# Selected values travel with the NSA pages, four MoBA columns among the pairs, transposes parted

## What is computed

```python
z = x @ w_in                       # one projection, split among four head groups
# A  conformer convolution (256 channels)
# B  native sparse attention, 4 heads, one K/V head per branch:
kc, vc = nsa_compress(rows[:, :, 0]), nsa_compress(rows[:, :, 1])   # compressed branch
# selected branch: blocks of 64 rows of rows[:, :, 2:] (sel_k, sel_v), top 16 by importance
# window branch: the last 512 rows and the row itself
# C  MoBA, 4 heads, blocks of 256 keys, top 3 and the own block
# D  multi-scale causal pooling
x = LN(ALPHA * x + concat(A, B, C, D) @ w_out)
x = LN(ALPHA * x + relu(x @ w_up)**2 @ w_down)
```

## Time and profile before

| | us |
|---|---|
| median of 3 runs | 766.06 (770.39, 765.99, 766.06) |
| profiled execution, device time | 770.32 |
| its span in the profile | 768.6 |
| PE busy | 737.8 |
| DVE busy | 429.2 |
| ACT busy | 285.5 |
| POOL busy | 210.4 |

### The profile page before, as it was taken

One profiled execution on the slowest core, in us unless ns is written; L12 is line 12 of the kernel. 1 busy time (PEld: TensorE's weight loads), 2 busy tenths in 40 slices (PEclk: granted clock), 3 DMA queues, 4 the chain that ended last, 5 costly groups with the idle time before them and its releaser, 6 DMA issues.

```text
span 768.6 us, 17343 instructions
## 1 busy us (share of the span) xinstructions
PE 737.8 (96%) x6904; PEld 659.2 (86%) x6904; DVE 429.2 (56%) x740; ACT 285.5 (37%) x561; POOL 210.4 (27%) x284
## 2 busy tenths in 40 slices
PE   8999999998987899999999999999999999999997
PEld 7999989875563545589999999999999999999996
DVE  4878994665643532556866556433563355536355
ACT  5222334465553222533434454212341124324115
POOL 0000527024226772004747721001110012100433
PEclk9999999999999899999999999999999999999999
DMA  9656773378779996321332333322233323325002
GB/s 332 188 151 182 213 200 97 133 286 315 280 252 309 261 280 208 117 83 56 130 144 84 89 104 104 117 83 84 83 104 93 106 71 95 107 87 165 2 15 99
DMA packets 63980, 113.49 MB, mean 148 GB/s; under 512 B 17017, under 2 KB 36218, under 8 KB 63226
## 3 DMA queue, kind: packets, MB, share of 16 engines
q1 hardware_dynamic: 57370, 95.58, 39.9%
q0 software_dynamic: 6528, 16.78, 6.7%
HBM read 107.90 MB, written 6.52 MB: 149 GB/s over the span
## 4 chain that ended last, share of the span: by engine, by line
PE 76%; DVE 8%; DMA 5%; issue 5%; SPq 4%; ACT 3%; POOL 0%; ACTq 0%; DVEq 0%; POOLq 0%
PE psum L793 55%; DMA moba_hi<-in_moba_pages 4%; PE psum L812 4%; PE psum L820 3%; PE psum L899 2%; PE psum L933 2%; SPq L707 1%; PE psum L1085 1%; SPq L629 1%; PE psum L868 1%; PE psum L1097 1%; DVE yc L1700 1%; DVE wL L1630 1%; PE psum L1133 1%; DMA wgate<-in_w_gate 1%
## 5 line engine op out<-in xcount | busy, mean ns | idle before, releaser
L1630 DVE TENSOR_TENSOR wL<-raw,wH 128x1024 fp32r<-128x1024 f32 (+1 forms) x85 | 107.1, 1261 | 84.2 <-ACT wH L1258 84.2
L1258 ACT ACTIVATE wH<-raw 128x1024 fp32r<-128x1024 f32 (+1 forms) x87 | 88.8, 1021 | 103.1 <-PE psum L793 101.1
L793 PE MATMUL psum<-oxH,wH 128*128 128x260 f32 (+1 forms) x512 | 105.0, 286 | 0.7 <-DVE oxL L2054 0.5
L793 PE MATMUL psum<-oxH,wL 128*128 128x260 f32 (+1 forms) x512 | 103.9, 284 | 0.0
L793 PE MATMUL psum<-oxL,wH 128*128 128x260 f32 (+1 forms) x512 | 103.4, 283 | 0.0
L1592 POOL TENSOR_TENSOR hsq<-relu 128x520 f32<-128x520 f32 x32 | 33.8, 1055 | 217.9 <-ACT relu L1437 217.9
L793 PE MATMUL psum<-opH,wH 128*128 128x260 f32 x400 | 85.5, 295 | 5.2 <-DVE wL L1630 1.4
L793 PEld LDWEIGHTS psum<-oxH,wH 128*128 128x128 f32 x512 | 79.5, 189 | 2.5 <-issue 1.7
L793 PE MATMUL psum<-opL,wH 128*128 128x260 f32 x400 | 80.5, 283 | 0.0
L793 PE MATMUL psum<-opH,wL 128*128 128x260 f32 x400 | 80.5, 283 | 0.0
L793 PEld LDWEIGHTS psum<-oxL,wH 128*128 128x128 f32 x512 | 79.9, 190 | 0.0
(11 more groups left out here) (395 smaller groups left out, 1313.1 us busy)
## 6 DMA issues: line engine op xcount, KB each, us to landing
raw<-in_panels SPq DMA_DIRECT2D x88, 512.0 KB, 3.6
nsa_ring<-in_nsa_pages SPq DMA_DIRECT2D x128, 96.0 KB, 2.2
moba_hi<-in_moba_pages SPq DMA_DIRECT2D x36, 256.0 KB, 5.2
moba_lo<-in_moba_pages SPq DMA_DIRECT2D x36, 256.0 KB, 5.3
moba_hi<-in_moba_pages POOLq DMA_DIRECT2D x28, 256.0 KB, 5.1
moba_lo<-in_moba_pages POOLq DMA_DIRECT2D x28, 256.0 KB, 5.5
xres<-in_xT SPq DMA_DIRECT2D x8, 260.0 KB, 5.2
xres<-in_xT SPq DMA_DIRECT2D x1, 2080.0 KB, 8.6
```

The source lines that it names most:

```text
L793: last = mm(out[:, hf, 0:cols], w, x[:, k, hf * HALF:hf * HALF + cols], start=(t == 0 and j == 0), stop=(t == KT - 1 and j == 2))
L1258: fn(wtiles(0, n).rearrange("p a b -> p (a b)")[:, cols], raw[:, n % NRAW, cols], ACT.Copy).then_inc(h_done, 1)
L1630: tt(wtiles(1, n).rearrange("p a b -> p (a b)")[:, cols], raw[:, n % NRAW, cols], wtiles(0, n).rearrange("p a b -> p (a b)")[:, cols].bitc ...
```

## The change

- `nsa_pages` grows to 256 columns: the selected values ride with the pages. w1's reserve shrinks from 16384 to 8192 bytes a partition, so the larger ring ends where it ended.
- In step `("nsa", b)` ACT first waits for the pages and copies their last 64 columns into `stage` (two buffers over `Vn` and `zs`); POOL writes `stage` (512 KB) to an internal DRAM tensor, `selv_rows[b]`. The next load into the ring waits for the copy too.
- `("selv", b)` is one load of 512 KB by SP, one for each sample, 5 units of time apart; POOL loads none.
- `zcols`, which fills `Vn`, waits for all write-backs; the convolution's temporary moves to `taps_tmp`.
- `NAHEAD` = 22: columns 18 to 21 (MoBA, first pair of heads) move among the pairs. They use banks 4 and 5 alone; from column 22 on odd columns use banks 0 and 3.
- `("st", b, 1)` is due 1.6 units after `("st", b, 0)`, not 2.5, and `("spv", b)` at 5.9, not 6.5. With the denser columns the merged order has other steps between the transposes.
- `comb_sub` and `comb_exp` become one semaphore.

```diff
+NAHEAD = sum(c[0] != "moba" for c in COLS) + 4
 def col_banks(n):
-    return (0, 3) if COLS[n][0] == "moba" and n % 2 else (4, 5)
+    return (0, 3) if n >= NAHEAD and n % 2 else (4, 5)
...
-MB1, PAIR_T, SELV_T = 9, 9.1, 6
-SELV_POOL = (1, 3, 5, 7)
-SELV_AT = [8 * (_m // 8) + (_m % 8) // 2 + 4 * (_m % 2) for _m in range(4 * B)]
-NCN = sum(c[0] != "moba" for c in COLS)
+MB1, PAIR_T, SELV_T = 9, 9.1, 5
...
         units += [(at_, ("mu", g)), (at_ + 2.5, ("mt", g)), (at_ + 4.7, ("mp", g))]
-        units += [(at_ + 4.6 * (m >= 4), ("selv", k)) for m, k in enumerate(SELV_AT[SELV_T * (g - MB1):SELV_T * (g - MB1 + 1)])]
     end = 1 + PAIR_T * (MB - MB1)
+    units += [(1 + SELV_T * b, ("selv", b)) for b in range(B)]
...
-        join += [(at_ - 3, ("psc", b))] + [(at_ + 2.5 * c, ("st", b, c)) for c in range(2)] + [(at_ + 6.5, ("spv", b))]
+        join += [(at_ - 3, ("psc", b))] + [(at_ + 1.6 * c, ("st", b, c)) for c in range(2)] + [(at_ + 5.9, ("spv", b))]
...
-        at_ = 3.2 + (end - 6.2) / NCN * n if n < NCN else end + 1 + 2.5 * (n - NCN)
+        at_ = 3.2 + (end - 6.2) / NAHEAD * n if n < NAHEAD else end + 1 + 2.5 * (n - NAHEAD)
...
-        at[0] = o_a + 16384
-        nsa_ring = place("nsa_ring", [P, 2, PAGES, 192])
+        at[0] = o_a + 8192
+        nsa_ring = place("nsa_ring", [P, 2, PAGES, 256])
...
+        selv_rows = nc.dram_tensor("selv_rows", [B, P, PAGES, HD], F32, kind="Internal").ap()
...
+        stage = place("stage", [P, 2, PAGES, HD], F32, o_vn)
+        taps_tmp = place("taps_tmp", [P, B, CW], F32, o_vn + 8192)
...
                         sp_.wait_ge(ssel_mm, n - 1)
+                        sp_.wait_ge(packed, n - 1)
...
-                elif kind == "selv" and n // 4 not in SELV_POOL:
+                elif kind == "selv":
                     if n == 0:
                         sp_.wait_ge(mm_done, N_IN_PANELS)
-                    for p, v in enumerate(pages(4 * n, 4), 4 * n):
-                        sp_.dma_start(selV[p // PAGES][:, p % PAGES, :],
-                                      a["selv_pages"][bass.ds(v, 1)].rearrange("a p n -> (a p) n")).then_inc(selv_in[p // PAGES], 16)
+                        for done in selv_out:
+                            sp_.wait_ge(done, 16 * B // 2)
+                    sp_.dma_start(selV[n][:, :, :], selv_rows[n]).then_inc(selv_in[n], 16)
...
-                first = min(m for m in range(NC) if COLS[m][0] == "moba" and m % 2)
+                first = min(m for m in range(NAHEAD, NC) if m % 2)
...
+                    if idx:
+                        act.wait_ge(nsa_in[n % 2], 16 * PAGES * (n // 2 + 1))
+                        if n == 0:
+                            act.wait_ge(gate_mm, 1)
+                        if n >= 2:
+                            act.wait_ge(selv_out[n % 2], 16 * (n // 2))
+                        fn(stage[:, n % 2, :, :], nsa_ring[:, n % 2, :, 192:256], ACT.Copy).then_inc(packed, 1)
                     act.wait_ge(cmp_mm, idx + 1)
...
+                    for done in selv_out:
+                        act.wait_ge(done, 16 * B // 2)
...
+                if kind == "nsa":
+                    pool.wait_ge(packed, n + 1)
+                    pool.dma_start(selv_rows[n], stage[:, n % 2]).then_inc(selv_out[n % 2], 16)
...
-        "nsa_pages": f(np.concatenate([cmpT, selK], 2)),
-        "selv_pages": f(nsa[:, :, 3]),
+        "nsa_pages": f(np.concatenate([cmpT, selK, nsa[:, :, 3]], 2)),
```

More of the change, by code:

```diff
@@ L583, in build @@
         shift_low = sem("shift_low_done")
+        packed, selv_out = sem("selv_packed"), [sem(f"selv_written_back{i}") for i in range(2)]
         pool_d, pool_mm = sem("pool_d"), sem("pool_mm")
@@ L592, in build @@
             sem("ms_mm"), sem("mmax"), sem("mt_mm"), sem("mp_mm"), sem("om_done"))
-        stat_mm, comb_sub, comb_exp, wb_done, back_mm = (
-            sem("stat_mm"), sem("comb_sub"), sem("comb_exp"), sem("wb_done"), sem("back_mm"))
+        stat_mm, comb, wb_done, back_mm = (
+            sem("stat_mm"), sem("comb_sub_then_exp"), sem("wb_done"), sem("back_mm"))
         pscaled, st_mm, spv_mm, md_done, mpv_mm, fin_o, fin_mm = (
@@ L663, in _ @@
                     sp_.wait_ge(ssel_mm, B)
+                    sp_.wait_ge(packed, B)
                     sp_.wait_ge(kc_done, B + 1)
@@ L1142, in _ @@
                         mm(psum[:, 3, :], zeros[:, :], Psel[:, 0, :], start=True, stop=False, skip_group_check=True)
[L1143 removed]
+                    pe.wait_ge(selv_in[b], 16)
                     pe.wait_ge(win_in, 32)
@@ L1392, in _ @@
                 elif kind == "combe" and n == 0:
-                    act.wait_ge(comb_sub, 1)
+                    act.wait_ge(comb, 1)
                     fn(sm[:, 0:NGATE], zs[:, 0, 0:NGATE], ACT.Tanh, scale=0.5)
                     fn(eb[:, 2, :, 0:33], eb[:, 2, :, 0:33], ACT.Exp)
-                    fn(eb[:, 2, :, 50:55], eb[:, 2, :, 50:55], ACT.Exp).then_inc(comb_exp, 1)
+                    fn(eb[:, 2, :, 50:55], eb[:, 2, :, 50:55], ACT.Exp).then_inc(comb, 1)
                 elif kind == "combe" and n == 1:
-                    act.wait_ge(comb_sub, 2)
-                    fn(eb[:, 2, :, 33:50], eb[:, 2, :, 33:50], ACT.Exp).then_inc(comb_exp, 1)
+                    act.wait_ge(comb, 3)
+                    fn(eb[:, 2, :, 33:50], eb[:, 2, :, 33:50], ACT.Exp).then_inc(comb, 1)
                 elif kind == "backa":
@@ L1703, in _ @@
                     if n == 0:
-                        tmp = Vn[:, 0, :, :].rearrange("p a b -> p (a b)")[:, 0:B * CW].rearrange("p (b k) -> p b k", b=B)
+                        tmp = taps_tmp[:, :, :]
                         for t in range(2):
@@ L1903, in _ @@
                             last = tt(E[:, :, lo:hi], spread(MN[:, br, :], hi - lo), NM[:, :, lo:hi], ALU.subtract)
-                        last.then_inc(comb_sub, 1)
+                        last.then_inc(comb, 1)
                     elif n == 1:
                         if kind == "comba":
-                            dve.wait_ge(comb_exp, 1)
+                            dve.wait_ge(comb, 2)
                             ts(sm[:, 0:NGATE], sm[:, 0:NGATE], 0.5, 0.5, ALU.mult, ALU.add)
                         else:
-                            dve.wait_ge(comb_exp, 2)
+                            dve.wait_ge(comb, 4)
                         for br, (lo, hi) in parts:
```

8 lines of the change are left out of this document (removed).

## The result

The changed kernel took 772.17 us (median of 20 runs, 766.83 to 777.12). The kernel before took 767.84 us (median of 20). The ratio is 1.0053, 95% interval 1.0038 to 1.0067: slower by about 4 us, less than the 1% that the prediction took as the border of "no change", and outside the forecast range of 753.5 to 767. The sign was wrong too: -8.5 us were added up, +4.3 us came.

A forecast was written before the change was run, and what follows sets the result against it. PE, busy 96% of the span, was taken as the bound, with DMA holding part of the MoBA stage. Stage -6.4, tail -3.1 and packing +1.0 gave -8.5 us; the middle of 761.8 and 757.6 was put at 759.6, range 753.5 to 767.

The forecast's parts named there:

- NSA periods, cost 0 (bound 5): 11.03 us periods of compressed and selected keys: longer pages and write-backs fit, DMA demand 10.9 us; cost 0, bound 5 us.
- NSA periods overflow: Rival, chance 0.10: in the NSA periods additions move at 145 GB/s, demand 15.0 us, 19 us lost after slack, 779 us.
- ACT packs, +1.0: ACT's eight copies in the NSA periods: hidden except the last sample's, which adds 1.0 us (0.4 to 2.1) to the path.
- The stage, -6.4: Last eight MoBA pairs, 228.00 to 311.38 us: page waits and most low clock go, four columns enter; 77.0 instead of 83.4 us.
- The tail, -3.1: 311.38 to 331.05 us, after the last pair: fewer columns queue ahead of DVE's chain; -3.1 us, bounds -1.5 and -3.8.
- What comes after is unchanged: From the first output panel at 331.05 us on, the change costs and saves nothing.
- The profile against the median: Whole execution: profiled 770.32 against median 766.06 us; whether the 4.3 us lay in the stage was undecided, so the middle was taken.

The follow-up runs named there:

- the repairs: Changed kernel with ACT's last two samples' copies moved earlier: 769.55 us; kernel before with parted transposes, two columns moved, six in tail 3.4 units apart: 765.22 us.
- e13: Changed kernel with the eight write-backs issued by ACT right behind its copy instead of by POOL: 776.23 us, ratio 1.0111 to the kernel before.
- e1: Kernel before with only the four MoBA columns moved and the transposes parted, selected values still in 128 small loads: 766.94 us, ratio 0.9989.
- e3: Changed kernel without ACT's copy, the write-back and their waits, selected values read from weight panels (wrong values): 769.58 us, ratio 1.0031 to the kernel before.
- e6: Changed kernel without the write-back, ACT's copy and its waits kept, selected values read from weight panels (wrong values): 770.86 us, ratio 1.0042 to the kernel before.
- e10: Kernel before with one more ACT copy of 128x1024, into free space, at the head of the last sample's step: 769.63 us, ratio 1.0032.

## Why the prediction was wrong

The steps stand in the order of the execution. Those that the repairs confirm in the time are ACT's copy with the clock behind it (2.6 us) and the idle time and clock ahead of panel 17 (2.0 us).

- **NSA periods, cost 0 (bound 5): wrong, the first step to fail.** It cost 0 to 4 us, by execution. The step compared the demand on the DMA engines (10.9 us) with the period. That demand was not even reached (0.87 x 11.0 = 9.6 us). What had no room was SP's round: 9.2 us of issues, the panel and the page numbers in a period of 11.03. The rows for it were at hand (67.02 and 9.22 in the earlier trace rows), but I used them only for the slack of one sample, and took an issue's duration as fixed. With the write, long issues became three times as many. The rival "NSA periods overflow" named the right place with the wrong resource and a size (19 us) far too large. Its point of decision, 11.8 us of demand, was never reached.
- **ACT packs, +1.0: right in size, wrong in what follows.** Panel 11 to 13 grew by 0.9 us in all profiles with the copy in its place (1.8 in e13, where ACT issues the write too). But the copy lengthened PE's wait ahead of panel 13 from 1.2 to 2.1 us, and the sum had no term for the clock behind a *new* wait, though it counted 5.1 us of clock behind old ones. The sum put that term at nothing, without a reason. It is 2.9 us in both profiles of the changed kernel; taking the copy away gave 2.6 us in the time.
- **The stage, -6.4.** In the first two profiles mu 9 to the end of the last pair went from 81.5 to 77.4 us, -4.1. The missing part is the DMA wait: I kept 1 us, and 3.9 (second profile 4.8) are there, for a pair whose pages are issued around the outputs, as before (4.1). The page wait was put down to selV's small descriptors; e1 kept them and has the same stage (164.6 us from the first pair to panel 17) as e3 with eight large loads (164.2). What the DMA engines had to do did fall: shares of 0.76 and 0.65 (windows 229.86:331.05 and 237.67:332.21) are 77 and 61 us, so 15 of the 18 us worked out are gone. It just wasn't what PE waited for: behind 228 us PE waits 2 to 7 us for MoBA pages in every profile, with small loads and without. The 3.4 us on ACT's copy did go.
- **The tail, -3.1.** 17.1 us instead of 19.7: -2.6, within the bounds. "What comes after is unchanged" is where it failed: with no columns behind mpv, PE idles 2.28 + 0.92 us and panel 17 starts at 1.2 GHz, +1.9 us on average, and +1.1 to +2.2 in every profile with four moved columns, where the five with none moved take 437.3 to 437.6 us.
- **The profile against the median.** The 4.3 us between 770.32 and 766.06 were shared out evenly. Of before's 20 runs the median is 767.84, and the second profile has a stage 2.8 us shorter: most of those us were the stage's own bad luck, which a change can't give back. e1 shows it: 5.3 us better in its profile, 0.3 in the median. (The middle of 757.6 and 761.8 is 759.7, not 759.6; nothing hangs on it.)

What was not settled: which part of the packing's own 2.6 us belongs to longer reads, to the write and to the large loads; what columns and parted transposes each gain; why e13 is so slow; and why the clock fell behind 2.1 us of waiting in e6 and not in e10.

## What to carry to other kernels

Before adding bytes to a stretch that PE hides, look at the *issuing* queue's round against the period, not only at the share of the DMA engines: a round whose engine waits only 1.9 us in all over five rounds has next to no slack, and here extra traffic made more of the issues long. Price every new wait of PE twice, once for itself and once for the clock behind it, and ask of each block of work that is moved away which wait it was filling: here two columns left in the tail and spread around mpv and finm gave some 2 us over four moved columns. A single profile of either kernel may be 2 to 5 us off its median, so a gain of that size is to be read from many runs and from stretches that repeat in several profiles.

## What the runs showed of the hardware

- The length of an idle time near 2 us did not by itself decide PE's clock behind it: idle 2.1 to 2.5 us ahead of panel 13 was followed by 1.2 GHz in 6 of 7 profiles (4.06 us in the eighth as well), 1.2 us in 1 of 12, and the stretch of low clock cost 1.5, 2.9 or 7.5 us.
- A DMA issue of SP is not of fixed length. In the same timeline single issues take 0.33 and 2.66 us (DMA share 0.92 during the latter). With 512 KB written per period 8 to 12 of 80 issues took over 0.5 us, without 2 to 4 of some 84. A high share is not needed: in the kernel before one took 1.71 us at a share of 0.40 (58.48 to 60.20 us).
- Periods with page runs of 1 KB moved little faster than with runs of 768 bytes: in one of e3 231 GB/s at a share of 0.80, or 289 at a full one, against 192 at 0.71, or 270; whole MoBA pages reach 388 at 1.01. Each period also holds a weight panel, and the issues differ in size too (96, 128 and 256 KB), so that the length of a run is the cause is not shown. The Trainium skill (DMA: Bandwidth & Descriptors, Specifications) puts line rate at 512 bytes and more; these rows don't agree.
- 512 KB written took 5.1 us to land (median of eight, issued by POOL) and 512 KB read back among the MoBA pages 9.9 us, where a weight panel of the same size takes 3.6.
